# A decoder layer's last stage: the gate product by Strassen's scheme over pairs of row tiles

## What is computed

```python
def channel_and_ple(x, p_i, ...):
    h = rmsnorm(x, norm_moe_g).reshape(B * S, D)
    x = x + hier_moe(h, ...).reshape(B, S, D)
    gate = jax.nn.sigmoid(rmsnorm(x, norm_ple_g) @ w_ple_gate + b_ple_gate)
    e = rmsnorm(p_i @ w_ple_proj, norm_ple_post_g)
    return x + gate * e

y_prompt = rmsnorm(xp, norm_final_g)
```

## Time and profile before

| | |
|---|---|
| median of 3 runs | 1866.74 us (1863.59 to 1871.02) |
| the profiled execution's own time | 1864.51 us |
| its span | 1862.8 us, mean granted TensorE clock 0.972 |
| busy share: TensorE, VectorE, ScalarE, GpSimd | 94%, 31%, 16%, 10% |
| the last stage | from about 1709 us to the end |

### The profile page before, as it was taken

One profiled execution on the slowest core, in us unless ns is written; L12 is line 12 of the kernel. 1 busy time (PEld: TensorE's weight loads), 2 busy tenths in 40 slices (PEclk: granted clock), 3 DMA queues, 4 the chain that ended last, 5 costly groups with the idle time before them and its releaser, 6 DMA issues. The chain is left out here.

```text
span 1862.8 us, 26448 instructions
## 1 busy us (share of the span) xinstructions
PE 1746.3 (94%) x10375; PEld 872.8 (47%) x10375; DVE 575.8 (31%) x1161; ACT 305.8 (16%) x548; POOL 194.3 (10%) x307
## 2 busy tenths in 40 slices
PE   8999999999999997988799997999998999995997
PEld 4564554556566663444464444433333334331443
DVE  4301104433334454566232226211011101111565
ACT  2000001222222223322210104100000000000122
POOL 1000004200000002333100000100000000001330
PEclk9999999999999997999899998999999999997999
DMA  8012110344344629999632145799999999999341
GB/s 288 5 16 91 49 51 1 107 153 170 123 168 162 228 90 324 353 377 375 238 115 80 68 175 216 291 378 427 428 427 427 427 426 427 385 426 356 113 151 64
DMA packets 133165, 427.19 MB, mean 229 GB/s; under 512 B 24153, under 2 KB 62618, under 8 KB 120754
## 3 DMA queue, kind: packets, MB, share of 16 engines
q1 hardware_dynamic: 98242, 327.59, 46.2%
q0 software_dynamic: 19488, 68.21, 9.9%
q10 hardware_dynamic: 15312, 29.70, 4.2%
HBM read 373.09 MB, written 52.37 MB: 228 GB/s over the span
## 5 line engine op out<-in xcount | busy, mean ns | idle before, releaser
L2303 PE MATMUL psum<-arena 128*32 128x512 f32 (+2 forms) x2144 | 312.4, 594 | 3.8 <-issue 2.3
L902 PE MATMUL psum<-arena 128*128 128x384 f32 (+1 forms) x768 | 253.9, 476 | 2.9 <-ACT arena L933 2.9
L2303 PEld LDWEIGHTS psum<-arena 128*32 128x32 f32 (+2 forms) x2144 | 99.0, 118 | 184.4 <-issue 180.7
L902 PEld LDWEIGHTS psum<-arena 128*128 128x128 f32 x768 | 139.9, 191 | 76.6 <-issue 5.8
L2342 PE MATMUL psum<-arena 128*32 128x512 f32 (+2 forms) x1072 | 159.0, 607 | 15.0 <-issue 14.0
L1692 PE MATMUL psum<-arena 128*128 128x512 f32 x256 | 114.7, 604 | 1.6 <-PEq L1513 1.6
L2662 PE MATMUL psum<-arena 128*128 128x512 f32 x256 | 113.7, 602 | 1.4 <-DVE arena L2688 1.4
L317 PE MATMUL psum<-arena 128*128 128x512 f32 x256 | 112.6, 597 | 0.4 <-DMA arena<-in_w_in 0.4
L2342 PEld LDWEIGHTS psum<-arena 128*32 128x32 f32 (+2 forms) x1072 | 53.4, 120 | 117.8 <-issue 117.8
L2397 DVE TENSOR_TENSOR arena<-psum,g_moe_rows 128x1024 f32<-128x1024 f32 x22 | 26.9, 1225 | 250.0 <-PE psum L2297 250.0
L2662 PEld LDWEIGHTS psum<-arena 128*128 128x128 f32 x256 | 48.9, 194 | 60.0 <-issue 60.0
(11 more groups left out here) (309 smaller groups left out, 1861.5 us busy)
## 6 DMA issues: line engine op xcount, KB each, us to landing
arena<-in_w_exp_gate SPq DMA_DIRECT2D x32, 2048.0 KB, 16.6
arena<-in_w_exp_up SPq DMA_DIRECT2D x32, 2048.0 KB, 17.1
arena<-in_w_exp_down SPq DMA_DIRECT2D x32, 2048.0 KB, 17.0
arena<-in_cache_v POOLq DMA_DIRECT2D x128, 256.0 KB, 9.2
arena<-in_cache_k SPq DMA_DIRECT2D x124, 256.0 KB, 9.7
arena<-in_w_in SPq DMA_DIRECT2D x24, 1024.0 KB, 6.2
moe_out<-arena POOLq DMA_DIRECT2D x5, 2560.0 KB, 11.9
moe_out<-arena ACTq DMA_DIRECT2D x22, 512.0 KB, 12.0
```

The lines of the kernel that those rows point to most:

```text
L902: done = mm(c.bank[7][:, 0:b - a], WG[blk % 2][:, k, q * P:(q + 1) * P], HT[p // NCOL][:, k, :], start=(k == 0), stop=(k == KD - 1))
L2303: last = mm(out[rows_, :], XT[:, u % 2, k, rows_], c.ring_tile(LOAD[kind, r])[:, k, :], start=(k == 0), stop=(k == KD - 1))
```

## The change

Tiles are taken in pairs a = 2i, b = 2i + 1. With the pair's rows as the two rows of a 2x2 block matrix X (its columns are the two halves of the inner dimension) and the weights W as 2x2 blocks W11, W12, W21, W22 of 512x512, the four result blocks come from seven block products of four matmuls each (`times`), where the plain form has eight. The order on TensorE is P1 = X11 W11, P6 = S2 T2, P4 = X22 T4, transposes of tile a + 2, P7 = S3 T3, P5 = S1 T1, transposes of b + 2, P2 = X12 W21, P3 = S4 W22. P7 is added in bank_b to P6, P2 in bank_a to P1, P3 in bank_c to P5.

- T1 to T4 (512x512 each) are differences of weight blocks, made once by VectorE (`mix_w`), S1 to S4 differences of tile halves, made for each pair (`mix_x`, `mix_last`).
- ScalarE copies P1 to `X1`. VectorE makes U2 = P6 + P1 and, after P7, U3 = U2 + P7 (`sum_u2`, `sum_u3`).
- GpSimd makes U2 rstd_a + bias, U3 rstd_b + bias for either half (`scaled_sum`, a TENSOR_SCALAR and a TENSOR_TENSOR over 128x512 each, three times a pair). VectorE's `gate` then makes product times rstd plus that term for each of the four result blocks (g11, g12 for tile a, g21, g22 for b), in place of `biased`.
- Tile b is finished ahead of a (`ORDER`). `EP` is gone: `weighted_e` writes in place in `E`. SyncE loads the projection's rows of the next pair when both tiles of a pair are multiplied, in a queue in which the store of tile b stands ahead.
- The sample tile's product is unchanged and stands last, in bank_a.

```diff
-    EP = view(c, W_AT + 4 * D, 2, D)
-    XT = view(c, W_AT + 6 * D, 2, KD, P)
+    T3 = view(c, W_AT + 4 * D, KD // 2, 512)
+    XT = view(c, W_AT + 6 * D, 2, KD, P), view(c, W_AT + 12 * D, 2, KD, P)
...
+    X1, U2, U3, W21 = [view(c, at + n * 512, 512) for n in range(4)]
...
+    left = [a for a in SPARE[1:] if a not in (LAST_AT, LAST_AT + WBLK)]
+    T1, T2 = [view(c, left[0] + n * 2 * D, KD // 2, 512) for n in range(2)]
+    T4 = view(c, left[1], KD // 2, 512)
+    S1, S2, S3, S4 = [view(c, left[1] + 2 * D + n * 512, KD // 2, P) for n in range(4)]
+    W11, W12, W21_, W22 = [c.wpg[n % 2][:, 4 * (n // 2):4 * (n // 2) + 4, :] for n in range(4)]
+    bank_a, bank_b, bank_c, bank_d = c.bank[0:4]
...
+    IN_PAIR = {"P1": 1, "P6": 2, "P4": 3, "P7": 4, "P5": 5, "P2": 6, "P3": 7}
+    ORDER = [t ^ 1 for t in range(NP)] + [NP]
...
-            for t in range(NT):
-                if 1 <= t and t + 1 < NT:
-                    sp.wait_ge(ep_done, t)
-                    load_e(t + 1)
-                sp.wait_ge(y_done, t + 1)
+            for t in ORDER:
+                if t % 2 == 0 and t < NP:
+                    sp.wait_ge(t_done, t + 2)
+                    load_e(t + 2)
+                    if t + 3 < NT:
+                        load_e(t + 3)
+                sp.wait_ge(y_done, nth(t))
...
+            def scaled_sum(out, x, t, half, done, n):
+                g.tensor_scalar(out, x, ST[:, 0, 2, t:t + 1], None, ALU.mult).then_inc(done, 1)
+                pool.wait_ge(done, n + 1)
+                g.tensor_tensor(out, out, bias_row[:, 512 * half:512 * half + 512], ALU.add).then_inc(done, 1)
...
+            for t in range(2):
+                gather(t + 2)
                 power(0, t)
-                gather(t + 2)
-            for t in range(NT):
-                if t + 2 < NT:
-                    power(0, t + 2)
-                    gather(t + 4)
-                power(1, t)
+            for i in range(NB2):
+                a, b = 2 * i, 2 * i + 1
+                pool.wait_ge(u_done, 2 * i + 1)
+                scaled_sum(U2, U2, a, 1, w12_done, 2 * i)
+                for t in (a + 4, b + 4):
+                    gather(t)
+                for t in (a + 2, b + 2):
+                    if t < NT:
+                        power(0, t)
+                pool.wait_ge(u_done, 2 * i + 2)
+                scaled_sum(W21, U3, b, 0, w2_done, 4 * i)
+                scaled_sum(U3, U3, b, 1, w2_done, 4 * i + 2)
+                power(1, b)
+                power(1, a)
+            power(1, NP)
...
+            square(0, 1)
+            for i in range(NB2):
+                a, b = 2 * i, 2 * i + 1
+                act.wait_ge(product, produced(i, "P1"))
+                if i:
+                    act.wait_ge(u_done, 2 * i)
+                s.activation(X1, bank_a, ACT.Copy).then_inc(p1_kept, 1)
+                for t in (a + 2, b + 2):
+                    if t < NT:
+                        square(0, t)
+                act.wait_ge(g21, i + 1)
+                act.wait_ge(g22, i + 1)
+                sigmoid(b)
+                act.wait_ge(g11, i + 1)
+                act.wait_ge(g12, i + 1)
+                sigmoid(a)
+                square(1, b)
+                square(1, a)
+            act.wait_ge(g_last, 2)
+            sigmoid(NP)
+            square(1, NP)
...
+            def times(bank, x, w, start):
+                for k in range(KD // 2):
+                    last = mm(bank, x[:, k, :], w[:, k, :], start=start and k == 0, stop=k == KD // 2 - 1,
+                              skip_group_check=True)
+                last.then_inc(product, 1)
...
-                pe.wait_ge(x_kept, t + 1)
-                if t >= 2:
-                    pe.wait_ge(bias_done, t - 1)
-                if t < NP:
-                    for half in range(2):
-                        for k in range(KD):
-                            last = mm(gate_ps[t % 2][:, half * 512:half * 512 + 512], XT[:, t % 2, k, :],
-                                      c.wpg[half][:, k, :], start=(k == 0), stop=(k == KD - 1))
-                        if half == 0:
-                            turn_x(t + 1)
...
+                pe.wait_ge(x_kept, a + 1)
+                if i:
+                    pe.wait_ge(g11, i)
+                times(bank_a, xt(a)[:, 0:4], W11, True)
+                pe.wait_ge(w_mixed, 4)
+                pe.wait_ge(s_mixed, 4 * i + 2)
+                if i:
+                    pe.wait_ge(u_done, 2 * i)
+                times(bank_b, S2, T2, True)
+                if i:
+                    pe.wait_ge(g21, i)
+                pe.wait_ge(x_kept, b + 1)
+                times(bank_d, xt(b)[:, 4:8], T4, True)
+                turn_x(a + 2)
+                pe.wait_ge(s_mixed, 4 * i + 3)
+                pe.wait_ge(u_done, 2 * i + 1)
+                times(bank_b, S3, T3, False)
+                if i:
+                    pe.wait_ge(g12, i)
+                times(bank_c, S1, T1, True)
+                turn_x(b + 2)
+                pe.wait_ge(p1_kept, i + 1)
+                times(bank_a, xt(a)[:, 4:8], W21_, False)
+                pe.wait_ge(s_mixed, 4 * i + 4)
+                pe.wait_ge(g22, i + 1)
+                times(bank_c, S4, W22, False)
+            pe.wait_ge(x_kept, NT)
+            pe.wait_ge(g11, NB2)
+            for k in range(KD):
+                for half in range(2):
+                    last = mm(bank_a[64 * half:64 * half + NS, :], xt(NP)[:, k, 0:NS], c.wpg[half][:, k, :],
+                              start=(k == 0), stop=(k == KD - 1))
+            last.then_inc(last_mm, 1)
...
+            def mix_w():
+                for out, x, y in ((T1, W12, W11), (T2, W22, T1), (T3, W22, W12), (T4, W21_, T2)):
+                    if y is T1:
+                        dve.wait_ge(w_mixed, 1)
+                    if y is T2:
+                        dve.wait_ge(w_mixed, 2)
+                    v.tensor_tensor(out, x, y, ALU.subtract).then_inc(w_mixed, 1)
...
+                v.tensor_tensor(S1, a2[:, 0:4], a2[:, 4:8], ALU.add).then_inc(s_mixed, 1)
+                dve.wait_ge(s_mixed, 4 * i + 1)
+                v.tensor_tensor(S2, S1, a1[:, 0:4], ALU.subtract).then_inc(s_mixed, 1)
+                v.tensor_tensor(S3, a1[:, 0:4], a2[:, 0:4], ALU.subtract).then_inc(s_mixed, 1)
...
+                v.tensor_tensor(U2, bank_b, X1, ALU.add).then_inc(u_done, 1)
...
+            def gate(done, bank, t, half, rest):
+                v.scalar_tensor_tensor(out=G[:, t % 2, 512 * half:512 * half + 512], in0=bank, scalar=ST[:, 0, 2, t:t + 1],
+                                       in1=rest, op0=ALU.mult, op1=ALU.add).then_inc(done, 1)
...
+            dve.wait_ge(c.final_in, 16 * 5)
+            mix_w()
...
+            mix_x(0)
+            mix_last(0)
+            for i in range(NB2):
+                a, b = 2 * i, 2 * i + 1
+                if i:
+                    y(b - 2)
+                x2(a + 2)
+                sum_u2(i)
+                if i:
+                    y(a - 2)
+                x2(b + 2)
+                weighted_e(a)
+                sum_u3(i)
+                keep_x(a + 2)
+                weighted_e(b)
+                dve.wait_ge(product, produced(i, "P5"))
+                dve.wait_ge(w2_done, 4 * i + 4)
+                dve.wait_ge(rstd[0], b + 1)
+                gate(g22, bank_c, b, 1, U3)
+                gate(g21, bank_d, b, 0, W21)
+                keep_x(b + 2)
+                mix_x(i + 1)
+                dve.wait_ge(product, produced(i, "P2"))
+                gate(g11, bank_a, a, 0, bias_row[:, 0:512])
+                x3(b)
+                dve.wait_ge(product, produced(i, "P3"))
+                dve.wait_ge(w12_done, 2 * i + 2)
+                gate(g12, bank_c, a, 1, U2)
+                mix_last(i + 1)
+                x3(a)
+            y(NP - 1)
+            weighted_e(NP)
+            y(NP - 2)
...
```

More of the change, by code:

```diff
@@ L2568, in stage_final, with nth, xt, produced @@
     x_tr, x_kept = c.sem("x2_tr"), c.sem("x2_kept")
-    gate_mm, bias_done, sig_done, ep_done, t_done, x3_done, y_done = (
-        c.sem(n) for n in ("ple_gate_mm", "ple_bias", "ple_sig", "ple_ep", "ple_t", "x3_done", "yf_done"))
+    product, last_mm, w_mixed, s_mixed = c.sem("ple_product"), c.sem("ple_last_mm"), c.sem("w_mixed"), c.sem("x_mixed")
+    p1_kept, u_done, w12_done, w2_done = c.sem("p1_kept"), c.sem("u_done"), c.sem("w12_done"), c.sem("w2_done")
+    g11, g12, g21, g22, g_last = (c.sem(f"gate_{n}") for n in ("g11", "g12", "g21", "g22", "last"))
+    sig_done, ep_done, t_done, x3_done, y_done = (c.sem(n) for n in ("ple_sig", "ple_ep", "ple_t", "x3_done", "yf_done"))
+    def nth(t):
+        return ORDER.index(t) + 1
+    def xt(t):
+        return XT[t // 2 % 2][:, t % 2]
+    def produced(i, name):
+        return 7 * i + IN_PAIR[name]
     with nc.Block() as block:
@@ L2645, in turn_x @@
             def turn_x(t):
+                if t >= NT:
+                    return
                 pe.wait_ge(x2_done, t + 1)
@@ L2651, in turn_x @@
```

(55 more changed lines are left out.)

84 lines of the change are left out of this document (37 added, 47 removed).

## The result

The change makes the kernel slower: 1886.95 us in the median of 4 runs (1884.89 to 1888.97) against 1867.41 for the kernel before on the same chips, a ratio of 1.0106 with a 95% interval of 1.0086 to 1.0125. The profiled execution took 1884.89 us, 20.4 more than that of before.

The account below looks back on a forecast made before the run. GpSimd's passes and gathers, not TensorE, were taken to bound the last stage: 1755 + 97 + 26.3 = 1878.3 for the last y, 18.8 us later. The profiled 1864.5 becomes 1883.3, the median 1885.5; range 1874 to 1894.

Parts of the forecast that it names:

- TensorE's part: Last stage: four pairs save one block product of 3.43 us each, 13.7 us in all, if TensorE stays the bound.
- The loop: Last stage, GpSimd's passes and gathers with VectorE's work set the pace: loops of 35, 33 and 29 us, together 97.
- W: The moment in a pair when GpSimd's fourth pass over U3 is done, for which g22 waits; first one put at 1755.
- The mis-sized term: GpSimd's TENSOR_SCALAR over 128x512, taken as 1.27 us like TENSOR_TENSOR, 1.3 with semaphores; upper end 1.67.
- The cheap pass: Rival: GpSimd's TENSOR_SCALAR takes 0.6 us, twelve passes on the path save 8 us, giving 1877.5; chance 0.23.
- Shutting out: Rival: GpSimd and VectorE don't shut each other out in this stage, 10.5 us less, 1875; chance 0.10.
- The lower clock: Rival: TensorE's half pace after waits isn't hidden, U2 up to 3 us later in three pairs, 1894; chance 0.12.
- TensorE stays the bound: Rival: fourth pass done when P3 is due, W to W at most 25.8 us, 13.7 us won, 1864; chance 0.08.
- The rival's second figure: In the rival where TensorE stays the bound: 1857 us if the 4.0 us at the start are hidden too.
- The start: Stage start: weight mixing and gathers delay P1 to 1727.3 from 1723.3, 4.0 us; first W at 1755.
- The end: From the last W to the last y 26.3 us, about 4.2 of the slowdown from the late load of the sample tile's rows.
- edits at nothing: Edits counted as free: P1's copy, S operations, rstd, and next-pair row loads (up to 1 us if they land late).

Follow-up runs that it names:

- e1: The changed kernel without GpSimd's six passes a pair, gates taking U2 and U3 as they are (work left out): 1863.62 us in one run.
- e4: The changed kernel with the three scaled sums of a pair made on VectorE, one fused operation each: 1863.12 us median, ratio 0.9968 to the kernel before.
- e7b: The changed kernel with scaled sums on VectorE and the sample tile's rows loaded early, mixing left in place: 1857.20 us, ratio 0.9948 to the kernel before.
- e10: The changed kernel with GpSimd's three TENSOR_SCALAR a pair multiplying by the number 1.0 instead of each partition's factor: 1884.63 us in one run.
- e3: The changed kernel with GpSimd's gathers of a pair placed behind the passes over U3: 1874.74 us median, ratio 1.0042 to the kernel before.
- e9: The changed kernel with the scaling of the sums done on ScalarE as three copies, GpSimd keeping the three additions: 1870.19 us in one run.
- e6b: The changed kernel with the weights' mixing moved behind the first two tiles' residual sums and turning, cut in two: 1891.69 us in one run.
- e5: The changed kernel with the sample tile's projection rows loaded early into a free gather buffer: 1884.24 us in one run.
- e7: The changed kernel with scaled sums on VectorE, the sample tile's rows loaded early and the mixing moved: 1861.28 us, ratio 0.9970 to the kernel before.

## Why the prediction was right, point by point

The forecast of 1885.5 us stands 1.5 below the median, and the mechanism held: GpSimd's passes bound the loop. That the number came so close is in part luck. From the first gather to the end of the last y the prediction had 167.7 us (1878.3 less 1710.57), and the trace has 167.7 (1879.56 less 1711.85), since a start put 1.1 too long and loops put 1.0 too short cancel.

- **TensorE's part.** 224 instructions, 25.8 us a pair when nothing holds it (e1, e4). The instructions saved exist. The change wins none of the 13.7 us. e7b wins 11.0 by its medians (1868.19 less 1857.20) and 8.0 counted from the first gather (152.2 less 144.2), so up to 3 us of the difference of medians may lie in the stages ahead.
- **The loop.** 35, 33, 29 predicted, 35.7, 33.5, 28.8 measured. In the second pair: W to the end of `power(1, b)` 12.5 predicted, 12.5 measured (1755.03 to 1767.54); U2's sum done at 17.0, and 16.9; U2's passes done at 21.6, and 22.0; gathers 5 to 6.5, and 6.1; two `power` 1.9, and 1.8; four passes 5.2, and 5.8. TensorE's waits ahead of P3 were put at 4, 8, 6 and 2 and are 3.7, 6.8, 5.3 and 1.2; VectorE's ahead of g22, put at 5 to 8, are 7.5, 9.8, 7.5 and 4.1.
- **The mis-sized term.** TENSOR_SCALAR over 128x512 was put at 1.27 us, the duration of TENSOR_TENSOR. It takes 1.56 alone. The slope of the two small TENSOR_SCALAR rows gave 1.67, which I had kept as the upper end, and was nearer: the same operation in another size told more than another operation in the same size. Over twelve passes this is 3.5 us. It doesn't show in the total, since other terms had room: the loops took 98.0 for 97, the term of 35 standing at the upper end of its own 34 to 35, and the first g22 came 43.3 us after the gather's start where 1755 less 1710.57 is 44.4, with 1.3 in it for collisions that weren't needed.
- **The cheap pass** (rival, 0.23) fell with e10: 1.49 us at the least. The Trainium skill, GPSIMD Engine Reference, section Engine selection, calls one-input operations there roughly line-rate. The rows speak against it: with one input the pass takes 1.57 us, with two 1.26.
- **Shutting out** (rival, 0.10) fell with the rows above: 1.28 became 2.32 on VectorE, 1.57 became 3.64 on GpSimd. The Trainium skill, SBUF — State Buffer, section SBUF: two separate sides, has it as an exclusive lock of a port pair for a VectorE operation with two SBUF inputs against a GpSimd operation that reads SBUF. The runs agree, as far as they show the two kinds side by side: in e10 1.49 became 2.46.
- **The lower clock** came as the trace of before had it and was hidden, as counted: in the second pair U2's sum started on time although TensorE ran at 0.50 for 6 us. In e3 and e4, where TensorE waits less, an instruction's mean is 597 and 604 ns, before the change 602, in the change 638.
- **TensorE stays the bound** (rival, 0.08) would have needed a W by the time P3 was due. e3 shows how near the order of one queue brings it, e4 reaches it by another engine. e3 and e9 together, with GpSimd still making the additions, were not run: 30.7 less the 5.2 that e3 gained is an estimate of 25.5 for the first loop, just under TensorE's 25.8. The rival's second figure is a wrong sum: 1864 less the 4.0 at the start is 1860, not 1857.
- **The start.** P1 at 1727.3 predicted, 1728.3 in a trace whose stage began 1.3 later: right. Counted from the first gather P1 came at 16.5 us, where in the kernel before the first product came at 12.8 (1723.32 less 1710.57), so the 4.0 us are 3.7. e6b gives 2.5 of them back, the part of the mixing.
- **The end.** 26.3 predicted, 26.4 measured, and e5 shows that the 4.4 us wait was for the load: 3.9 of it came back. A second wait for rows, 1.39 us at 1843.72, is the "up to 1 us if not" of the prediction's edits at nothing.

## What to carry to other kernels

When a scheme trades TensorE's work for elementwise work, look for the engine whose queue the new work joins, and walk one turn of the loop with everything that already stands in that queue: here some 10 us a pair went in where 3.4 came out. Elementwise passes on GpSimd beside a busy VectorE cost more than their own time on both; the same sums as fused operations on VectorE cost a quarter. Before moving work off the start of a stage, ask whose wait it lay in, and which product the slowest chain begins with.

## What was not expected of the hardware

- GpSimd's TENSOR_SCALAR over 128x512 is slower (1.56 us) than its TENSOR_TENSOR (1.26), and reading the factor for each partition costs 0.07 us alone, but 1.2 us (3.64 for 2.46) in the two pairs in which VectorE's operations follow each other without a gap, and 0.07 (2.53 for 2.46) in the two in which they don't.
- The issue of a gather took 0.94 us alone, 1.9 to 2.4 beside VectorE's mixing in the change and e7b, and 2.84 once in e7, more than the 1.42 of the earlier trace rows. Where the mixing stood elsewhere (e6b), the first four issues took 0.94 each. This is the issue of e7, beside a mixing from 1729.71:

```profile
1729.97 2.84 POOL L2629 DMA_INDIRECT arena<-moe_out,arena  x1 [0.30 <-issue]
```

- The span of the stages ahead of the changed one differs by several us from run to run, as much as some of the edits are worth.
